# Another order of the 63 experts in a mixture-of-experts stage on one Trainium2 core

## The reference, cut to what matters

```python
def swiglu(x, w_gu, w_down):
    gate, up = jnp.split(x @ w_gu, 2, axis=-1)
    return (jax.nn.silu(gate) * up) @ w_down
...
    y = swiglu(x_pad[tok], w_gu[ex], w_down[ex])
    return acc.at[tok].add((y * wt[:, None]).astype(acc.dtype)), None
```

## Time and profile before

| | us |
|---|---|
| median of 3 runs (2417.1 to 2418.42) | 2418.12 |
| profiled execution, its own time | 2438.98 |
| span of the profiled execution, first to last instruction | 2437.1 |
| expert stage in it, place 0 to place 62 | 1578 to 2374 |

### The profile page before, as it was taken

How to read it: one execution, slowest core, us unless ns; L and a number is a source line. 1 busy time by engine, 2 the same in 40 slices (tenths; PEclk the granted TensorE clock), 3 DMA queues, 4 the chain that set the end, 5 groups by cost and what they waited for, 6 DMA issues and landing times.

```text
span 2437.1 us, 24693 instructions
## 1 busy us (share of the span) xinstructions
PE 2335.2 (96%) x8889; PEld 1341.9 (55%) x8889; DVE 1086.0 (45%) x1832; ACT 427.2 (18%) x692; POOL 793.8 (33%) x747
## 2 busy tenths in 40 slices
PE   6999999999999999999999999999999999999992
PEld 3784554444698344444445544466666656566652
DVE  5533554765765544565486442323222222223224
ACT  1001223335333011111102100011111111111112
POOL 3000111102452000000000046366767676676752
PEclk9999999999999999999999999999999999999996
DMA  6211003102002011110241520599999999999975
GB/s 249 109 36 68 1 35 109 52 9 79 1 2 87 26 52 61 52 52 26 67 175 43 194 70 3 173 362 346 347 324 348 311 342 326 329 345 346 337 230 171
DMA packets 168617, 383.55 MB, mean 157 GB/s; under 512 B 22268, under 2 KB 42976, under 8 KB 167345
## 3 DMA queue, kind: packets, MB, share of 16 engines
q1 hardware_dynamic: 136512, 304.87, 34.7%
q0 software_dynamic: 30976, 70.08, 11.6%
q10 hardware_dynamic: 1008, 7.02, 0.7%
HBM read 325.87 MB, written 66.58 MB: 161 GB/s over the span
## 4 chain that ended last, share of the span: by engine, by line
PE 94%; DMA 2%; DVE 1%; issue 1%; ACT 1%; POOL 0%; SPq 0%; DVEq 0%; POOLq 0%; ACTq 0%
PE banks L2253 13%; PE banks L1570 12%; PE banks L2261 9%; PE banks L332 9%; PE banks L2294 8%; PE banks L1582 6%; PE banks L420 6%; PE banks L2231 5%; PE banks L460 5%; PE banks L2124 4%; PE banks L325 2%; PE banks L2109 2%; PE banks L1045 1%; PE banks L1027 1%; PE banks L2218 1%
## 5 line engine op out<-in xcount | busy, mean ns | idle before, releaser
L2826 POOL DMA_INDIRECT arena<-hp_scratch,arena x300 | 306.2, 1021 | 202.8 <-issue 94.3
L2253 PE MATMUL banks<-arena 128*128 128x136 f32 (+8 forms) x2240 | 321.3, 304 | 16.7 <-issue 13.1
L2253 PEld LDWEIGHTS banks<-arena 128*128 128x128 f32 x2240 | 312.4, 195 | 24.3 <-issue 20.7
L1570 PE MATMUL banks<-arena 128*128 128x512 f32 x672 | 292.9, 596 | 1.5 <-DVE arena L1697 1.5
L2261 PE MATMUL banks<-arena 128*128 128x512 f32 (+1 forms) x528 | 238.6, 595 | 2.5 <-ACT arena L2432 1.6
L332 PE MATMUL banks<-arena 128*128 128x512 f32 x512 | 224.2, 593 | 0.3 <-ACT arena L547 0.3
L1570 PEld LDWEIGHTS banks<-arena 128*128 128x128 f32 x672 | 128.1, 191 | 163.4 <-issue 162.9
L2294 PE MATMUL banks<-arena 128*128 128x512 f32 x464 | 204.8, 593 | 0.3 <-DVE arena L2689 0.3
L276 POOL TENSOR_SCALAR arena<-arena 128x1 f32<-128x1 f32 x16 | 10.0, 625 | 576.2 <-DVE arena L267 576.2
L2842 POOL DMA_INDIRECT acc_scratch<-arena x97 | 150.5, 1551 | 69.5 <-issue 41.4
L332 PEld LDWEIGHTS banks<-arena 128*128 128x128 f32 x512 | 95.3, 189 | 122.7 <-issue 117.0
(11 more groups left out here) (425 smaller groups left out, 2851.1 us busy)
## 6 DMA issues: line engine op xcount, KB each, us to landing
arena<-in_exp_w_gu SPq DMA_DIRECT2D x64, 2048.0 KB, 14.0
arena<-in_exp_w_down SPq DMA_DIRECT2D x64, 1024.0 KB, 16.2
arena<-in_w_in SPq DMA_DIRECT2D x10, 2048.0 KB, 8.4
arena<-in_w_in SPq DMA_DIRECT2D x12, 1024.0 KB, 5.7
arena<-in_w_branch SPq DMA_DIRECT2D x12, 512.0 KB, 6.8
hp_scratch<-arena SPq DMA_DIRECT2D x10, 512.0 KB, 2.7
acc_scratch<-arena SPq DMA_DIRECT2D x10, 512.0 KB, 4.5
arena<-hp_scratch,arena POOLq DMA_INDIRECT x300
```

Source lines behind the costliest of these rows:

```text
L1570: last = nc.tensor.matmul(PS[:, g % 4, :], lhs[:, k, :], rhs[:, k, :], start=(k == 0), stop=(k == 3))
L2253: last = nc.tensor.matmul(PS[:, bank + part, f * n:(f + 1) * n], weights[:, k, part * FF + f * P:part * FF + (f + 1) * P], x[:, k, 0:n], s ...
L2826: nc.gpsimd.indirect_dma_start(out=rows[0:n, :], out_offset=None, in_=table, in_offset=bass.IndirectOffsetOnAxis(ap=at, axis=0), bounds_ch ...
```

## The change

```diff
     at = {r: (i + 0.5) / len(double) for i, r in enumerate(double)}
-    at.update({r: i / (len(single) - 1) for i, r in enumerate(single)})
+    at.update({r: (i / (len(single) - 1)) ** 0.75 for i, r in enumerate(single)})
     return sorted(range(NE - 1), key=lambda r: (at[r], r)) + [NE - 1]
```

## The result

| | median, us | lowest to highest | ratio to before, 95% interval |
|---|---|---|---|
| before, measured again beside it (17 runs) | 2418.48 | 2415.4 to 2421.23 | 1 |
| after (17 runs) | 2424.61 | 2420.79 to 2428.36 | 1.0024, 1.0017 to 1.003 |
| predicted | 2417.0 | 2408 to 2427 | |

The new order is **slower by 6.1 us, 0.24%**. The range held the time. The forecast ("no difference that can be told", and if any then -1.8 us) didn't, and neither did its reasons.

A forecast was written before the change was run, and what follows sets the result against it. TensorE's steps plus 20 instruction-supply pauses were taken as the bound. Steps, weights and gathered rows counted 0 us, positions -1.8 us, scaled to -0.4 to -1.8 unrecorded; from a 2418.12 us median this gave 2417.0 us, range 2408 to 2427.

The forecast's parts named there:

- Term (3): Expert stage, rows gathered by GpSimd: no added wait, 0 us, with a cover of 2.35 us at place 42.
- term (4): Two-piece places just behind multiples of 256 instructions pause for instruction supply: 25.7 us after against 27.5 before, -1.8 us.
- those 20 pauses: TensorE's waits for "issue" in front of L2253 in the expert stage, 13.1 us in 20 pieces.
- Step 1: Expert stage, TensorE: same 63 places and tokens, each with its own `hidden` and `down`, sum unchanged, 0 us.
- Step 2: Expert stage, weights: landed about 14.0 us after issue, needed about 50 us after it, so no wait, 0 us.
- gathered rows come late: Rival: TensorE waits at places 1 to 3 with a DMA as cause; two or three waits make 2425; chance 0.05.
- the pauses belong to the recording: Rival: the recording causes 20.9 of 27.5 us of pauses or nearly so; order worth nothing, 2418.1 us; chance 0.15.

The follow-up runs named there:

- the second profile: The kernel before, profiled once more with no edit; 2417.97 us in the profiled execution.
- the adds first: GpSimd's adds of place r-4 issued ahead of the gathers of place r: 2426.91 us on after's order, 2418.2 us on before's.
- three pairs put back: After's order with places 36 and 37, 46 and 47, 56 and 57 exchanged, so two-piece places adjoin again; 2419.41 us, ratio 1.0003 to before.

## Why the prediction was wrong

Two terms of its sum failed. Term (3), rows gathered by GpSimd, stood at 0 us and hid the loop that makes after slower; term (4), the positions, stood at -1.8 us and was nothing. Term by term:

**What bounds the kernel** ("TensorE's steps plus those 20 pauses"): half right. The steps are the floor, and with half of the gate and up weights left out both orders stand at about 2409. But the 9 us above it in the kernel before are the full DMA engines, not the pauses. I had the warning in hand: the DMA share of 1.01, and a profiled execution 20.9 us above the median. I took that excess as a doubt about the *size* of one term. It was a doubt about every row of the trace, because in an execution with 27 us of pauses the weights keep their lead (45 us from issue to need in places 50 to 59, against 25), and so it hides the waits of the others.

**Step 1, TensorE's steps: 0 us.** Right. Both orders take 753.1 us from place 0 to 62 when the DMA is relieved.

**Step 2, weights: 0 us.** The reason was wrong. "Land about 14.0 us after issue" is the landing of one weight behind the stage; in the second profile it is 24.6 us. "Needed about 50 us later" is about true of the first profile, but in the second the issue is only 25 us ahead by places 50 to 59, and in places 51 to 61 the weights came late, 6.2 us in 7 waits. After has more lead in the middle (15.2 and 7.1 us in places 30 to 39 and 40 to 49, against 9.6 and 4.4) and doesn't wait for a gate or up weight. That isn't a gain of the order by itself: once the loop holds TensorE up, the weights have more time, and with the adds first the same order waits 13.7 us for them.

**Step 3, gathered rows: 0 us.** This is the step that failed and that turned the sign. I had "GpSimd is busy for 67%" and a cover of 2.35 us at place 42. Neither is about the adds, which stand in the same queue and the same loop. Measured: 10.7 us in eight waits in front of L2301 that the second profile of before doesn't have, and 3.3 us for ScalarE where before has 1.6. Less before's 6.2 us of waits for weights that is 6.2 us, near the 6.1 of the medians. The rival "gathered rows come late" was the nearest, at 2425 us with a chance of 0.05. Its price was right by luck: it put the wait at places 1 to 3 with a DMA as the cause, where after waits for nothing; the wait is at 40 to 58, where the order has *no* pair, and the page blames VectorE for it.

**Step 4, positions: -1.8 us.** It fell whole. After has the places 8, 37 and 51 at positions 6, 30 and 34, and none paused; nor did 2, 25, 39 and 53. This is place 8 of after, exactly the undisturbed 10.85 us of the earlier trace rows:

```profile
1684.39:1695.24 10.85, 10.85 (x75) 8.93 (x73) 2.67 (x5) 1.27 (x3) 8.36 (x8) 1.00 1.04 349
```

Before's order, profiled again with the same positions, had no pause either. The rival "the pauses belong to the recording" (0.15) was right about them and wrong about the time. The Trainium skill ("Runtime: NRT & Kernel Launch", section on instruction fetch) says that crossing a block of 256 instructions is mostly hidden; every profile but the first agrees. I had seen a real pattern, five of five, in one sample.

**What stays open.** What made the five pauses of the first profile isn't known; none of the twelve later profiles had more than one wait of 0.7 us for "issue" in the stage, so nothing here could be tried on it. How much of after's 6.1 us is loop and how much late weights can't be split cleanly either, since each covers the other: the loop alone is 3 to 4 us with an eighth less of the gate and up weights, the weights alone 6.9 us with the adds first. That the adjacent pairs let the loop recover rests on one order with three pairs put back. And no version here that loads all its weights beats the kernel before: the best, adds first on its own order, is 0.9993 with an interval that takes in 1.

## What to carry to other kernels

Before a wait in a trace gets a price, lay the profiled execution's own time beside the spread of the plain runs: where it lies outside, take no wait, and no *missing* wait, from it. Ask of a median how many transfers stand behind it, and of a queue not only whether it is late but whether its lead shrinks. Where the DMA engines are full next to a full TensorE, an order of work is judged by the slowest loop of DMA round trips that it must keep up with (here one add, the outputs, the next add, the gates and the gather, about 25 us a pair), and not by each engine's busy share. A perfectly even alternation may be the worse one: here three adjacent pairs of long steps gave 5 of 6 us back.

## What the runs showed of the hardware

- An indirect add to memory took 9.0 to 9.4 us from issue to landing in the rows above (median 9.3 in after) with a DMA share of 1.03, and two in sequence set a period of 24.0 to 25.8 us with the work between them. VectorE's wait for them, 219.4 us in all, cost TensorE nothing before place 40; in the second profile of before 175.6 us cost it nothing in front of the transposes.
- A gate and up weight of 2 MB took 24.6 us from issue to landing (median) in both orders at that share, and 16.2 and 16.7 us with an eighth left out. SyncE's queue held the issue of a `down` weight for 9 to 12 us late in the stage.
- Relief of one user of the DMA engines is taken by the next: 11.6 us of one wait fell to 0.9 us, and 13.7 us of another appeared.
- A third of the weights less (half of gate and up) is worth 0.37% (9 us) to before's order, and a twelfth less (an eighth of gate and up) 0.35%. The load is over the edge only by a little, but all through the stage: the weights' lead shrinks from 35.8 to 0.4 us, and only the last fifth of the places pays.
- One execution of the kernel before lost some 27 us in five places with the mean clock of three of them at 0.81 and 0.82, in groups of 4 matmuls every 1.43 us, and this was never seen again.
